# Asking for an expert's down weights from ScalarE instead of SP

## The reference

```python
logits = h @ w_router + b_router
top_v, top_e = lax.top_k(logits, 4)                  # 4 of 32 experts
gate = softmax(top_v)
def run_block(args):                                 # xb: tokens of one expert e
    xb, e = args
    gu = xb @ w_gu[e] + b_gu[e]                      # 1024 -> 2048
    gt = jnp.minimum(gu[:, :1024], 7.0)
    up = jnp.clip(gu[:, 1024:], -7.0, 7.0)
    act = (up + 1.0) * gt * jax.nn.sigmoid(1.702 * gt)
    return act @ w_dn[e] + b_dn[e]                   # 1024 -> 1024
```

## Time and profile before

| what | value |
|---|---|
| median of three runs | 1585.25 us |
| the profiled execution | 1591.11 us |
| its span, first to last instruction | 1589.2 us |
| PE busy | 1512.8 us, 95% |
| DVE, ACT busy | 486.3 us, 333.6 us |
| bytes moved by DMA | 541.31 MB, mean 341 GB/s |
| mean granted TensorE clock | 0.988 of full speed |
| loads of `w_gu` from SP | 126 of 2 MiB, median 23.7 us to landing |
| loads of `w_dn` from SP | 64 of 2 MiB, median 21.6 us to landing |

### The profile page before, as it was taken

One profiled execution on the slowest core, in us unless ns is written; L12 is line 12 of the kernel. 1 busy time (PEld: TensorE's weight loads), 2 busy tenths in 40 slices (PEclk: granted clock), 3 DMA queues, 4 the chain that ended last, 5 costly groups with the idle time before them and its releaser, 6 DMA issues.

```text
span 1589.2 us, 24547 instructions
## 1 busy us (share of the span) xinstructions
PE 1512.8 (95%) x9779; PEld 796.4 (50%) x9779; DVE 486.3 (31%) x1114; ACT 333.6 (21%) x795; POOL 6.7 (0%) x13
## 2 busy tenths in 40 slices
PE   5999989999999999999999999999999999999996
PEld 4888886776677688333333333333333333333332
DVE  1565566422301024322222222122222212222224
ACT  2333462222311103111112111111111111111113
POOL 0000000000000000000000000000000000000000
PEclk9998999999999999999999999999999999999999
DMA  9847541635399975599999999999999999999994
GB/s 395 332 159 326 217 162 78 233 133 168 129 322 363 343 300 178 223 386 426 429 428 428 429 429 429 428 428 428 429 428 428 429 428 429 429 427 428 428 428 182
DMA packets 60162, 541.31 MB, mean 341 GB/s; under 512 B 7202, under 2 KB 11810, under 8 KB 29250
## 3 DMA queue, kind: packets, MB, share of 16 engines
q1 hardware_dynamic: 59378, 534.65, 81.7%
q0 software_dynamic: 720, 5.76, 0.9%
HBM read 533.54 MB, written 6.84 MB: 340 GB/s over the span
## 4 chain that ended last, share of the span: by engine, by line
PE 60%; DMA 32%; DVE 4%; issue 1%; ACT 1%; SPq 0%; ACTq 0%; DVEq 0%
DMA ring<-w_gu 30%; PE banks L555 16%; PE banks L1318 9%; PE banks L601 6%; PE banks L869 5%; PE banks L1151 2%; PE banks L530 2%; PE banks L1083 2%; DMA ring<-wpre 2%; PE banks L802 1%; PE banks L967 1%; PE banks L1176 1%; PE banks L1337 1%; PE banks L1211 1%; PE banks L1355 1%
## 5 line engine op out<-in xcount | busy, mean ns | idle before, releaser
L555 PE MATMUL banks<-ring,regA 128*64 128x512 f32 x2024 | 451.1, 595 | 17.1 <-DMA ring<-w_gu 16.4
L555 PEld LDWEIGHTS banks<-ring,regA 128*64 128x64 f32 x2024 | 140.8, 137 | 304.0 <-issue 264.1
L601 PE MATMUL banks<-ring,regC 128*64 128x512 f32 x1024 | 226.8, 595 | 1.4
L663 DVE TENSOR_TENSOR regB<-regB,banks 128x528 f32<-128x528 f32 x128 | 81.5, 698 | 327.7 <-PE banks L530 327.7
L601 PEld LDWEIGHTS banks<-ring,regC 128*64 128x64 f32 x1024 | 71.6, 137 | 136.0 <-issue 127.8
L629 ACT ACTIVATE regA<-regA 128x512 f32<-128x512 f32 x32 | 20.2, 630 | 531.5 <-DVE regA L685 531.5
L685 DVE TENSOR_SCALAR regA<-banks 128x512 f32<-128x512 f32 x32 | 22.1, 691 | 351.0 <-PE banks L572 351.0
L505 PE MATMUL banks<-regC,regA 128*64 128x512 f32 (+1 forms) x396 | 98.5, 615 | 0.0
L869 PE MATMUL banks<-hT,ring 128*128 128x264 f32 x384 | 86.5, 387 | 0.0
L869 PEld LDWEIGHTS banks<-hT,ring 128*128 128x128 f32 x384 | 72.6, 190 | 12.8 <-issue 0.4
L530 PE MATMUL banks<-regA,regC 64*128 64x264 f32 x512 | 71.6, 409 | 0.0
(11 more groups left out here) (481 smaller groups left out, 1550.1 us busy)
## 6 DMA issues: line engine op xcount, KB each, us to landing
ring<-w_gu SPq DMA_DIRECT2D x126, 2048.0 KB, 23.7
ring<-w_dn SPq DMA_DIRECT2D x64, 2048.0 KB, 21.6
ring<-wpre SPq DMA_DIRECT2D x41, 2048.0 KB, 13.0
ring<-kvT SPq DMA_DIRECT2D x64, 256.0 KB, 4.8
ring<-kv SPq DMA_DIRECT2D x64, 256.0 KB, 6.2
ring<-ssm SPq DMA_DIRECT2D x2, 2048.0 KB, 10.7
o_ssms<-ring POOLq DMA_DIRECT2D x2, 2048.0 KB, 8.0
regC<-w_gu SPq DMA_DIRECT2D x1, 2048.0 KB, 12.0
```

The lines of the kernel that those rows point to most:

```text
L555: mm = pe_mm(bank[x // 2][SLOT * (x % 2):SLOT * (x % 2 + 1), :], lhsT=hg[:, k % 4, SLOT * (k // 4):SLOT * (k // 4 + 1)], rhs=weights_k[:, ...
L601: mm = pe_mm(bank[5][SLOT * y:SLOT * (y + 1), :], lhsT=actT[:, m % 4, SLOT * (m // 4):SLOT * (m // 4 + 1)], rhs=ring[c][:, D * (m % 4) + H ...
L663: V.tensor_tensor(pair, pair, banks[:, b:b + 2, 0:T], ALU.add).then_inc(acc_added, 1)
```

## The change

SP no longer asks for c4 and c5 after item 0. ScalarE asks for both, at the start of its item j (from item 1 on), behind one wait on `moe_read` for the end of item j - 1. As its queue runs in order, that is behind the copy (L641) of the result of item j - 1. SP's queue keeps c1, c2, c3 and the next c0. ScalarE's first item stands outside the loop now, and for items past 32 it reads the expert's number as SP does.

```diff
             def later_chunks(j, e):
-                for c in range(1, RING):
+                for c in range(1, 4):
                     sp.wait_ge(moe_read, j * 6 + (c - 5))
                     load(c, e)
...
-            for c in range(2, RING):
+            for c in range(2, 4):
                 sp.wait_ge(moe_read, c + 1)
                 load(c, 1)
...
-            for_items(act, 0, item)
+            def later_item(j, e):
+                act.wait_ge(moe_read, j * 6)
+                for c in range(4, RING):
+                    act.dma_start(ring[c][:, :], wdn[bass.ds(e, 1), c - 4, :, :].rearrange("a p n -> p (a n)")).then_inc(slot_in[c], 16)
+                item(j)
+
+            item(0)
+            with act.Fori(1, NE) as j:
+                later_item(j, j)
+            K = number_of_items(act)
+            with act.If(K > NE):
+                with act.Fori(NE, NJ) as j:
+                    with act.If(j < K):
+                        later_item(j, act.value_load(items[0:1, bass.ds(j + 1, 1)], min_val=0, max_val=NE - 1))
```

## The result

The changed kernel takes 1594.11 us (median of 13 runs), the kernel before 1586.01 (13 runs): a ratio of 1.0049, with a 95% interval of 1.0036 to 1.0062, that is 5.7 to 9.8 us slower. The forecast was 9.5 us. Two executions, one of e3 and one of the kernel before beside e7, took 3085.05 us, and the ratios in this document leave them out.

What follows compares the result with a forecast made beforehand. The prediction took DMA bandwidth (428 GB/s) to bound the expert loop; a late start of 4.1 us and a later c3 of 5.4 us, 9.5 us on the 1585.25 us median, gave 1594.75 us, range 1585 to 1604.

Steps and rivals of the forecast that it cites:

- The sum: Whole kernel: 4.1 and 5.4 us make 9.5 us, added to the median of 1585.25 us.
- What bounds the second part: Expert loop from 705 us: bytes over bandwidth at 428 GB/s, 29.4 us an item; TensorE 1.1 us an item faster.
- Instructions cost nothing: SP's and ScalarE's queues: moved issues and the table load out of the loop cost or gain 0 us.
- First term: Ahead of 705 us: c4 of item 2 asked for late, so unbroken loading starts late; +4.1 us, carried to the end.
- Second term: Expert loop: c3 lands later because c4 and c5 load beside it on their own queue; +5.4 us, ends 0 and 9.8.
- by halves: DMA engines: c4 and c5 get half of c3's 10.9 us, so c3 lands 5.4 us later; forecast given 50%.
- E + 1.8: Each item: E is the end of reading the former c5; ScalarE's chunks bring bytes about 1.8 us after it.
- It counts once, at the end: c3's 5.4 us lateness costs nothing more in mid-loop, only behind the landing of item 31's c3.
- One order for both queues: DMA queues: requests served as they come, only the late start of 4.1 us remains, 1589.35 us; 13%.
- ScalarE's or SP's chunks first: DMA queues: ScalarE's first, 13.9 us, 1599.1 us, 8%; SP's queue gets more, c5 late, 1627 us, 5%.
- another rate: DMA loading: two queues faster, 16% for a gain that matters; or slower by 1%, 1603.4 us, 8%.
- A chunk of down weights late for TensorE: Expert loop: TensorE waits for `w_dn` would show the forecast wrong; no size given.

Runs made afterwards that it cites:

- e3: Kernel before, but ScalarE asks for c4 and c5 of item 31 alone, behind the copy; ratio to the kernel before 1.0063.
- e7: Kernel before, all loads from SP, but c4 of items 2 to 21 asked for an item earlier, even items into buffer `ahead`; 1581.82 us, ratio 0.9976.
- e2: Kernel before, all loads on SP's one queue, but c4 and c5 asked for behind the copy of the former item's result; ratio to the kernel before 1.0022.
- e4: Changed kernel, but ScalarE asks for c4 and c5 of items 1 to 15 only, SP from item 16 on; ratio to the kernel before 1.0028.
- e1: Changed kernel, but ScalarE asks for c4 as soon as its slot is read, ahead of the copy, c5 behind it; ratio to the kernel before 1.0036.
- e5: Changed kernel, but SP asks for c4 and c5 of item 31, ScalarE for items 1 to 30; ratio to the kernel before 1.0058.

## Why the prediction was right

- *The time itself.* The sum was 1.5 us too large against the stretch (9.5 against 8.0). The absolute figure, 1594.75 us against 1594.11, came out nearer than that by luck: with more runs the median of the kernel before rose by 0.8 us. The span and the landing of the last c3 were forecast from one profiled execution, and the other one came to the experts 4.2 us sooner; from c3's landing to the end it is 33 us, as forecast.
- *What bounds the second part.* Right: 428 GB/s before and after, and lateness ahead of 705 us came out in full at the end of the loads, in both directions (4.1 us asked later and 3.9 us ended later in e2; 3.9 us ended sooner in e7).
- *Instructions cost nothing.* Right: ScalarE's busy time fell from 333.6 to 293.7 us with its table loads gone, and e4, whose ScalarE has these issues for 15 items, pays for the late start alone.
- *First term, 4.1 us.* Right in kind, 3.7 in size. I let ScalarE issue 0.2 us behind the end of its copy; it issues 0.46 us after the copy's start, while the copy still runs.
- *Second term, 5.4 us, by halves.* The mechanism holds (e1, e3), and so do the halves (c5 lands 9.8 us behind c4). The size was 4.3; the part that was mis-sized is when ScalarE's bytes begin. I let them begin 1 us behind the request, at E + 1.8. That 1 us holds where the engines are free: at c4(2), asked for at 699.95, there is no packet up to 700.75, and up to 701 us there are

```profile
q10 hardware_dynamic: 6, 0.10, 40.6%
```

  With q1 at work it is 3.3 us (rows of the DMA view above). The request itself leaves some 0.5 us behind E, so the bytes begin at E + 3.8, 2.0 us later than I had it, and half of that is 1.0 of the 1.1 us too much; why they begin later stays open. In e1 c4 is asked for 3.8 us earlier than in the changed kernel (51.6 against 55.4 us behind c0(2)) and runs beside c3 that much longer; half of it, 1.9, is near the 1.7 that its 6.0 has over 4.3. Both sizes are worked out from the rows, not tried. The Trainium skill ("DMA: Bandwidth & Descriptors", section "Queues, rings and completion order") has the engines go round their queues; the shares of 53 and 47% agree with it.
- *"It counts once, at the end."* The number holds, but the wording was too narrow: it is not the order of the last item's landings but a lag between TensorE and the loads, there from item 6 on, which one item in the old order does not remove (e5) and four do (e4).
- *The rivals.* One order for both queues fell with e3; ScalarE's or SP's chunks first, with the landings; another rate, with the windows. The Trainium skill (the same page, section "Issuing engines are not separate DMA queues") allows a second issuer nothing but sequencer time; the rate agrees.
- *A chunk of down weights late for TensorE.* The prediction called such waits a sign of being wrong. In the experts of the changed kernel there was one (us in total, times, longest), for c5 in item 5, whose copy came 28.26 us behind the one before all the same; so the margin was there, and thin:

```profile
PEld banks L601 <- DMA ring<-w_dn: 0.5, 1, 0.5
```

## What to carry to other kernels

When loads bound a loop and TensorE is nearly as fast, the time is set by when the unbroken stretch of loading starts and by how far TensorE's last tight chunk stands from the end of the bytes; ask of a changed order which chunk it puts in front of the tight one. A second queue lets later-needed chunks run beside sooner-needed ones, and one queue in the order of need does better here. A lag so made is worked off only at the difference of the two rates, so an order that fills holes at the start should be left several items ahead of the end.

## What the runs showed of the hardware that was not expected

- A DMA issue in ScalarE's queue does not wait for the copy ahead of it to end: 0.46 us after its start, of 0.60.
- The first bytes of a request came 0.8 to 1.1 us after its issue when the engines were free (c4(2) in the changed kernel), and 3.3 us after it when the other queue had work (c4 at 1136.46).
- In e3, around two waits of 4.3 and 4.4 us, TensorE's granted clock fell (0.57 to 0.88 in windows of 5 us, so partly at the lower of its two levels, 1.2 GHz), and c3's sixteen products took 5.92 us in place of 3.65. In the changed kernel, with items 0.5 and 1.7 us longer than TensorE needs by turns, it stayed at 1.00 from 705 to 1560 us.
